# Branch B of a hybrid attention block: weights packed in another order, exponentials and rotations kept in PSUM, two of eight transposes in other banks

## What is computed

```python
qb = rms_norm(b_cq, q_a_norm_w) @ w_q_b          # 512 -> 8 heads x (128 nope + 64 rope)
qb_rope = apply_rope(qb[..., 128:], cos_b, sin_b)
kvb = rms_norm(b_ckv, kv_a_norm_w) @ w_kv_b      # 256 -> 8 heads x (128 key + 128 value)
s = (q_nope @ k_nope.T + q_rope @ k_rope.T) * scale     # block-causal, 64-token chunks
out_b = softmax(s) @ v * silu(b_g)
x = x + concat(out_a, out_b) @ w_out             # then a last rms_norm
```

## Time and profile before

| | |
|---|---|
| median of 3 runs | 711.04 us (709.88 to 712.78) |
| the profiled execution | 710.97 us; its span from first to last instruction 709.0 us |
| PE busy | 682.3 us, 96% |
| DVE, ACT, POOL busy | 317.4, 303.0, 320.4 us (45%, 43%, 45%) |
| granted TensorE clock | 0.994 of full |

### The profile page before, as it was taken

The page is one execution under the profiler, slowest core; times in us unless marked ns, Lnnn a source line. Parts: engine busy times, 40 slices in busy tenths (PEclk is TensorE's granted clock), DMA queues, the critical chain, the costliest instruction groups (busy, mean ns, idle before and its releaser), DMA issues.

```text
span 709.0 us, 9019 instructions
## 1 busy us (share of the span) xinstructions
PE 682.3 (96%) x3282; PEld 567.3 (80%) x3282; DVE 317.4 (45%) x515; ACT 303.0 (43%) x573; POOL 320.4 (45%) x150
## 2 busy tenths in 40 slices
PE   5999999999999999999999998999999999999995
PEld 4888887888888888888888786778778888888884
DVE  5977120885753633543533666675752110100013
ACT  6732232212235564564554565566553231312233
POOL 3664443444254443344243255445675385474630
PEclk9999999999999999999999999999999999999998
DMA  8632222223132122222222222210111932232215
GB/s 277 232 126 101 101 89 90 90 91 115 61 119 90 60 84 80 100 70 85 90 89 80 100 86 77 76 61 31 59 60 61 355 119 94 90 113 89 90 52 215
DMA packets 21588, 73.47 MB, mean 104 GB/s; under 512 B 2352, under 2 KB 2480, under 8 KB 21424
## 3 DMA queue, kind: packets, MB, share of 16 engines
q1 hardware_dynamic: 18144, 66.07, 26.8%
q10 hardware_dynamic: 3408, 6.90, 2.7%
HBM read 68.77 MB, written 4.19 MB: 103 GB/s over the span
## 4 chain that ended last, share of the span: by engine, by line
issue 39%; PE 32%; POOL 18%; DVE 5%; ACT 3%; DMA 1%; POOLq 0%; ACTq 0%; SPq 0%; DVEq 0%
POOL w_lo L247 18%; PE bank L956 10%; PE bank L960 10%; PE bank L959 10%; DVE t L821 1%; DVE pb L862 1%; PE bank L1168 1%; DVE st_b L854 1%; DMA xs<-x_t 1%; DVE ptb_lo L867 1%; ACT pb L481 1%; PE bank L1159 0%; PE bank L1158 0%; DMA w_raw<-w_stream 0%; DVE mixed L766 0%
## 5 line engine op out<-in xcount | busy, mean ns | idle before, releaser
L247 POOL TENSOR_TENSOR w_lo<-w_raw,w_hi 128x1024 fp32r<-128x1024 f32 x109 | 265.2, 2437 | 319.3 <-ACT w_hi L320 318.6
L320 ACT ACTIVATE w_hi<-w_raw 128x1024 fp32r<-128x1024 f32 x110 | 116.1, 1059 | 216.3 <-PE bank L956 188.4
L956 PE MATMUL bank<-x_hi,w_hi 128*128 128x512 f32 x520 | 204.8, 394 | 0.0
L960 PE MATMUL bank<-x_lo,w_hi 128*128 128x512 f32 x520 | 202.9, 390 | 0.0
L959 PE MATMUL bank<-x_hi,w_lo 128*128 128x512 f32 x520 | 202.5, 389 | 0.0
L960 PEld LDWEIGHTS bank<-x_lo,w_hi 128*128 128x128 f32 x520 | 97.6, 188 | 20.5
L956 PEld LDWEIGHTS bank<-x_hi,w_hi 128*128 128x128 f32 x520 | 97.8, 188 | 20.1 <-DVE mixed L805 0.5
L959 PEld LDWEIGHTS bank<-x_hi,w_lo 128*128 128x128 f32 x520 | 97.7, 188 | 19.7 <-issue 0.5
L956 PE MATMUL bank<-w_hi,mx_hi 128*128 128x512 f32 x256 | 101.0, 394 | 0.0
L959 PE MATMUL bank<-w_hi,mx_lo 128*128 128x512 f32 x256 | 100.0, 391 | 0.0
L960 PE MATMUL bank<-w_lo,mx_hi 128*128 128x512 f32 x256 | 99.9, 390 | 0.0
(11 more groups left out here) (177 smaller groups left out, 909.8 us busy)
## 6 DMA issues: line engine op xcount, KB each, us to landing
w_raw<-w_stream SPq DMA_DIRECT2D x110, 512.0 KB, 3.2
xs<-x_t SPq DMA_DIRECT2D x8, 512.0 KB, 4.8
y<-x_nat ACTq DMA_DIRECT2D x4, 1024.0 KB, 8.8
out<-y SPq DMA_DIRECT2D x8, 512.0 KB, 3.4
fw<-final_w ACTq DMA_DIRECT2D x1, 1024.0 KB, 15.3
cos_b<-tables ACTq DMA_DIRECT2D x2, 256.0 KB, 2.7
sin_b<-tables ACTq DMA_DIRECT2D x2, 256.0 KB, 3.0
cos_r<-tables ACTq DMA_DIRECT2D x1, 256.0 KB, 3.3
```

Source lines behind the costliest of these rows:

```text
L247: pool.tensor_tensor(w_lo[:, s % HL, :], w_raw[:, s % RAW, :], w_hi[:, s % HL, :].bitcast(F32), ALU.subtract)\
L320: act.activation(w_hi[:, s % HL, :], w_raw[:, s % RAW, :], ACT.Copy).then_inc(w_hi_ready, 1)
L956: ins = pe.matmul(dst, ah, bh, start=start, stop=False)
L960: return pe.matmul(dst, ah, bl, start=False, stop=stop)
```

## The change

- The weights of a pair are packed as (rotary queries, keys), (other queries), (values, zeros) for all pairs, and the tiles come in the order 4, 0, 3, 5, 6, 1, 2 for all pairs. Before, pair 0 had the order 4, 5, 6, 0, 3, 1, 2 and the others 0 to 6.
- Tile 4 is projected in F0 and F1, and the rotation moves from F6 to F8 of DVE's walk to F2, F3 (three operations in each) and F4. The products with the cosine and the sum are written back to the PSUM bank of tile 4; before, they went to `t1` and `t3` in SBUF. That bank is free for the next tile (tile 6) only when the two last subtractions are done (`b_rot_lo`); before, after the multiplications.
- The exponential is written back to its score bank, and N reads it there. A score bank is free after N; before, after E. So S waits for N of two blocks earlier.
- T2 of each pair goes to bank 7 and T6 to bank 5; the others stay in bank 6, and T3 and T7 wait for the D of two blocks earlier, not of the last.
- The multiplication of the last two tiles of branch A by their gate (`gate(3)`) moves from DVE (before M2 of pair 0) to POOL, ahead of a weight chunk. The DMAs of the second pair of rotation tables, which go where the gate stood, are issued on ACT in F1 of pair 0; before in F3.
- Splits (ACT and POOL) of the tiles and of the chunks move with the new order; that of tile 2 falls into F0 of the next pair.

```diff
-B_PIECES = [((0, (0, 1)),), ((1, (0, 1)),), ((2, (0, 1)),), ((3, (0, 1)),), ((4, (0, 1)),), ((4, (2, 3)),), ((5, (0, 1)),),
-            ((5, (2, 3)),), ((6, (0, 1)),), ((6, (2, 3)),), ()]
+B_PIECES = [((4, (0, 1)),), ((4, (2, 3)),), ((0, (0, 1)),), ((3, (0, 1)),), ((5, (0, 1)),), ((5, (2, 3)),), ((6, (0, 1)),),
+            ((6, (2, 3)),), ((1, (0, 1)),), ((2, (0, 1)),), ()]
-TILE_ORDER = [(4, 5, 6, 0, 3, 1, 2)] + [(0, 1, 2, 3, 4, 5, 6)] * 3
+TILE_ORDER = (4, 0, 3, 5, 6, 1, 2)
-B_SPLITS = {1: 0, 2: 1, 3: 2, 4: 3, 8: 5, 10: 6}
-B_CHUNKS = {0: 0, 5: 1, 6: 2}
-B_ROTARY = {6: 0, 7: 1}
+B_SPLITS = {3: 0, 4: 3, 6: 5, 8: 6, 9: 1}
+B_CHUNKS = {1: 0, 5: 1, 10: 2}
+B_ROTARY = {2: (0, 1, 2), 3: (3, 4, 5)}
+B_ROTARY_HIGH, B_ROTARY_LOW = 4, 5
+T_BANK = (6, 6, 7, 6, 6, 6, 5, 6)
...
             def b_expo(w):
                 u = w % 8
                 n = P * (u % 4 + 1)
-                act.wait_ge(b_turned, w + 1)
                 act.wait_ge(b_max, w + 1)
-                act.activation(pb[:, u % 4, 0:n], B[4 + u % 2][:, 0:n], ACT.Exp, bias=st_b[:, u % 4, 0:1],
+                act.activation(B[4 + u % 2][:, 0:n], B[4 + u % 2][:, 0:n], ACT.Exp, bias=st_b[:, u % 4, 0:1],
                                accum_out=st_b[:, u % 4, 2:3]).then_inc(b_exp, 1)
...
             def b_rotary(p, part):
 
+                bk, own = B[(PB_TILES * p + TILE_POS[4]) % 4], min(p, 1)
                 if part == 0:
...
-                    if p > 0:
-                        dve.wait_ge(b_rot_lo, p)
-                    dve.tensor_tensor(t1[:, :], bk[:, :], cos_b[own][:, :], ALU.mult)
-                    for q in range(4):
-                        o = q ^ 1
-                        ins = dve.tensor_tensor(t2[32 * q:32 * q + 32, :], bk[32 * o:32 * o + 32, :], sin_b[own][32 * q:32 * q + 32, :], ALU.mult)
-                    ins.then_inc(b_rot_evac, 1)
+                if part < 4:
+                    o = part ^ 1
+                    dve.tensor_tensor(t2[32 * part:32 * part + 32, :], bk[32 * o:32 * o + 32, :], sin_b[own][32 * part:32 * part + 32, :], ALU.mult)\
+                        .then_inc(b_rot_evac, 1)
+                elif part == 4:
+                    dve.wait_ge(b_rot_evac, 5 * p + 4)
+                    dve.tensor_tensor(bk[:, :], bk[:, :], cos_b[own][:, :], ALU.mult).then_inc(b_rot_evac, 1)
                 else:
-                    dve.wait_ge(b_rot_evac, p + 1)
-                    dve.tensor_tensor(t3[:, :], t1[:, :], t2[:, :], ALU.add).then_inc(b_rot, 1)
+                    dve.wait_ge(b_rot_evac, 5 * p + 5)
+                    dve.tensor_tensor(bk[:, :], bk[:, :], t2[:, :], ALU.add).then_inc(b_rot, 1)
...
-                dve.tensor_scalar(pb[:, u % 4, 0:n], pb[:, u % 4, 0:n], st_b[:, u % 4, 3:4], None, ALU.mult).then_inc(b_probs, 1)
+                dve.wait_ge(b_turned, w + 1)
+                dve.tensor_scalar(pb[:, u % 4, 0:n], B[4 + u % 2][:, 0:n], st_b[:, u % 4, 3:4], None, ALU.mult).then_inc(b_probs, 1)
...
                 if j == 4:
-                    pe.wait_ge(b_rot_evac, p + 1)
+                    pe.wait_ge(b_rot_lo, p + 1)
...
-                pe.wait_ge(b_exp, w + 1)
+                if w >= 2:
+                    pe.wait_ge(b_probs, w - 1)
+                if w % 8 == 1 and w > 1:
+                    pe.wait_ge(b_pt_lo, w - 1)
...
                 pe.wait_ge(b_probs, w + 1)
-                pe.wait_ge(b_pt_lo, w + 1)
+                if T_BANK[w % 8] == 5:
+                    pe.wait_ge(b_probs, w + 2)
+                elif T_BANK[w % 8] == 7:
+                    pe.wait_ge(b_out, w // 4 + 1)
+                    pe.wait_ge(a_out, 17)
+                elif w > 0 and T_BANK[(w - 1) % 8] != 6:
+                    pe.wait_ge(b_pt_lo, w)
+                else:
+                    pe.wait_ge(b_pt_lo, w + 1)
...
-        parts = [np.concatenate([kn, v], axis=2), np.concatenate([qr, pad], axis=2), qn]
-        stream += parts[1:] + parts[:1] if p == 0 else parts
+        stream += [np.concatenate([qr, kn], axis=2), qn, np.concatenate([v, pad], axis=2)]
```

More of the change, by code:

```diff
@@ L190, in build, with turned @@
         B = [bank(f"bank{i}") for i in range(8)]
+        def turned(w):
+            u, n = w % 8, P * (w % 4 + 1)
+            return B[T_BANK[u]][:, 0:n]
         w_landed = [sem(f"w_landed{i}") for i in range(RAW)]
@@ L273, in _ @@
                 low_part(c, c)
-            with pool.Fori(1, b_head // HL) as i:
+            with pool.Fori(1, (b_head - 1) // HL) as i:
                 for s in range(HL):
                     low_part(HL * i + s, s)
-            for c in range(b_head // HL * HL, b_head):
+            for c in range((b_head - 1) // HL * HL, b_head):
+                if c == b_head - 1:
+                    for ct in range(2):
+                        pool.wait_ge(gate_silu, 12 + ct + 1)
+                        pool.wait_ge(a_out, 12 + 5)
+                        pool.tensor_tensor(mixed[:, 6 + ct, :], mixed[:, 6 + ct, :], gate_tmp[:, ct, :], ALU.mult).then_inc(gated, 1)
                 low_part(c, c)
@@ L281, in _ @@
                 for f in range(len(B_PIECES)):
+                    if p > 0 and f == 0:
+                        b_tile_low(p, 2)
                     if p < PAIRS - 1:
@@ L505, in _ @@
             act.wait_ge(w_used, PB0)
+            b_tile_high(0, 0)
+            b_tile_high(0, 3)
+            b_rotary_high(0)
+            high_part(PB0 + AHEAD, PB0 + AHEAD)
             b_tile_high(0, 5)
-            b_rotary_high(0)
             b_tile_high(0, 6)
[L509 to L512, removed]
+            high_part(PB0 + AHEAD + 1, PB0 + AHEAD + 1)
             preload(ACT.Exp)
@@ L525, in _ @@
                     elif step[0] == "F":
-                        if p == 0 and f == 3:
+                        if p > 0 and f == 0:
+                            b_tile_high(p, 2)
+                        if p == 0 and f == 1:
                             act.wait_ge(gated, 8)
@@ L873, in b_take @@
                 dve.tensor_tensor(m, B[7][:, :], m, ALU.mult).then_inc(b_out, 1)
-            for part in range(2):
+            for part in range(6):
                 b_rotary(0, part)
-            b_tile_low(5)
+            for j in (0, 3):
+                b_tile_low(j)
             b_rotary_low(0)
-            b_tile_low(6)
-            for j in (0, 3, 1, 2):
+            for j in (5, 6, 1, 2):
                 b_tile_low(j)
@@ L905, in _ @@
                         if p < PAIRS - 1:
-                            if f in B_ROTARY:
-                                b_rotary(p + 1, B_ROTARY[f])
-                            if f == 8:
+                            for part in B_ROTARY.get(f, ()):
+                                b_rotary(p + 1, part)
+                            if f == B_ROTARY_LOW:
                                 b_rotary_low(p + 1)
@@ L915, in _ @@
                         late = None
-                    if p == 0 and step == "F" and f == 2:
-                        gate(3)
             b_take(B_HEADS - 1)
@@ L1140, in b_project @@
                     for k in ks:
-                        o = step * k + (P if j in (3, 6) else 0)
+                        o = step * k + (P if j in (3, 6) else 0) + (SEQ if j in (0, 3) else 0)
                         if p == 0 and j == 4:
@@ L1174, in b_product @@
                 pe.wait_ge(b_out, head + 1)
-                if head == 0:
-                    pe.wait_ge(a_out, 17)
-                    pe.wait_ge(b_lo, 6)
+                if head % 2 == 0:
+                    pe.wait_ge(b_lo, 6 * (head // 2) + 6)
                 for kt in range(TOK):
@@ L1199, in out_rows @@
                     ins.then_inc(o_done, 1)
-            for j in TILE_ORDER[0]:
+            for j in TILE_ORDER:
                 b_project(0, j, (0, 1) if j < 4 else (0, 1, 2, 3))
@@ L1216, in _ @@
                         if p < PAIRS - 1:
-                            if p == 0 and f == 0:
+                            if p == 0 and f == 2:
                                 pe.wait_ge(b_lo, 6)
```

54 lines of the change are left out of this document (26 added, 28 removed).

## The result

The changed kernel takes **724.32 us** (median of 4 runs, 723.46 to 724.89) against 711.91 of the kernel before in the same runs (709.88 to 712.97): a ratio of 1.0173, with a 95% interval of 1.0156 to 1.019. It is 1.7% slower. The forecast was 712.4, with a range of 704 to 717. The profiled execution is at 724.89 us with a span of 723.0.

The account below looks back on a forecast made before the run. PE bounds the kernel, so only its idle time and clock can be won. 710.97 − 12.3 (waits, clock) − 1.2 (restarts) + 12.6 (new pair waits) + 0.3 (restarts) + 2.0 (tile 6) = 712.4 us; range 704 to 717.

Parts of the forecast that it names:

- the low parts of the rotation: DVE's subtractions right behind ACT's high parts, ahead of M5, N5 and D3, to 470.05; F6 starts 1.5 us late.
- The clock: Rival, 22%: PE's clock falls in the new waits, 1.7 us at most a fall, 716 us at 1.2 in three pairs.
- The rival with 23%: DVE isn't late enough to hold PE: 706 us with half the wait per pair, 699.5 with none; chance 23%.
- under 2 us at V0: Sign meant to decide for the 23% rival: V0 waits less than 2 us in a pair.
- The old waits: PE's waits for D, 9.5 us, and for a value tile, 1.1 us, from 412 to 545 us, were to go.
- The wait at tile 6: Ahead of pair 0, tile 6 waits for the rotation's end in tile 4's bank: 1.9 us, 2.0 with restart.
- S5: In pair 1, S5 waits for the 512 wide scaling from PSUM on DVE: 0.4 us.
- S6: In pair 1, S6 waits for the 128 wide scaling behind the rotation's products and sum: 1.2 us.
- those of F6 and V0: In pair 1, F6 waits 1.5 us for the rotation's low part and V0 0.9 us for D3.
- The gate: At T1 of pair 0, the gate on DVE causes the 3.53 us wait; on POOL it was costed at nothing.
- Writing PSUM in place: Rival, 9%: in-place PSUM writes cost 0.1 to 0.25 us on 18 operations, giving 714.2 to 717 us.
- The rule of the Trainium skill: Any PSUM operand slows a float32 tensor_scalar: 512 wide scaling at 0.69 us, not 0.49; 712.4 us with it, 711.2 without.

Follow-up runs that it names:

- e2: Changed kernel with the rotation's two last subtractions in F4 instead of F5: 713.35 us, ratio 1.0025 to the kernel before.
- e10: Changed kernel with the split of tile 3 in F5, behind E5, instead of F4: 721.18 us, ratio 1.0129 to the kernel before.
- e3: Changed kernel with 16 unread 512 wide matmuls right before the wait of F6 in pairs 0 to 2: 718.16 us, ratio 1.0084 to the kernel before.
- e8: Kernel before with gate(3) on POOL, T2 in bank 7, T6 in bank 5 and the exponentials in PSUM: 702.37 us, ratio 0.9866.
- e4: Kernel before with only gate(3) moved from DVE to POOL: 708.62 us, ratio 0.9944.
- e7: Kernel before with gate(3) on POOL, T2's transposes in bank 7 and T6 in bank 5: 704.93 us, ratio 0.9906.
- e1: Changed kernel with the rotation's products back in SBUF (t1, t3): 715.68 us, ratio 1.005 to the kernel before.
- e5: Changed kernel with the exponentials back in SBUF, S waiting for E of two blocks earlier: 726.7 us, ratio 1.0213 to the kernel before.
- e9: Changed kernel with the rotation's products in SBUF and the two last subtractions in F4: 711.52 us, ratio 0.9998 to the kernel before.
- e11: Changed kernel with the split of tile 3 in F5 and the rotation's subtractions in F4: 713.85 us, ratio 1.0025 to the kernel before.

## Why the prediction was wrong

**The step that failed** is the one on the low parts of the rotation: "ACT makes the high parts of the rotation behind E4 and H2, from about 467.4, and DVE the low parts right behind". DVE does not. `B_ROTARY_LOW` is 5: the subtractions stand in F5, behind M5, N5 and D3, and not, as the section on the change has it too, in F4. The prediction sent DVE through the subtractions first and then "M5 and N5 ... and D3". In the changed kernel the order is the reverse, and F6 waits for all five. With the order that was computed, F6 waits 1.11 us and V0 0.73 (e2). With the subtractions in F5, F6 waits 3.12 (e10), and the two copies of tile 3 ahead of E5 make it 3.99. V0 then waits for nothing. A pair loses 5.5 us instead of 4.1, which is 4.2 us over three pairs.

**The clock** was a rival with 22%, "between" single waits of 1.2 and 3.5 us. With 3.99 it is no longer between. The fall came in all three pairs, twice for double the time of the earlier trace rows, and costs 6.2 us in all, tile 6 included (e3). "A fall costs 1.7 us at most" was too low for that reason. The two together are 10.4 of the 11.9 us by which the forecast of 712.4 missed. The rest is in the terms below. The rival with 23%, that DVE isn't late enough to hold PE, is out: PE waits 5.5 us a pair, and 3.4 with the order that was computed. Its sign, under 2 us at V0, couldn't have told it from the sum, which had 0.9 there itself.

**What held.** The old waits went, at T1, T2, T6, T7 and at the value tile. The wait at tile 6 is 1.88 (1.9), S5 0.37 (0.4), S6 1.15 (1.2). The walk in time order thus was the right tool. Where its list of operations was right it had the waits to 0.1 us up to S6, and in e2 those of F6 and V0 0.4 and 0.2 too long.

**What was mis-sized, and partly cancelled.** In e2 the four waits of a pair sum to 3.36 us, not 4.1, yet the time is 0.95 over the forecast. Busy time of PE in pair 2, from S0 to S0, of e2 and of e8 (columns of rows 1), shows where that went:

```profile
481.56:513.00 31.44, 28.13 (x167) 23.32 (x166) 19.63 (x43) 18.73 (x42) 17.11 (x11) 1.00 0.15 51
```

```profile
472.96:502.05 29.09, 27.56 (x165) 23.35 (x165) 20.60 (x42) 18.83 (x43) 17.38 (x10) 1.00 0.16 55
```

The same pair's work is 0.57 us longer with four waits than with two, so a restart costs 0.2 to 0.3 us, also after a short wait. The rows say where it lies: a matmul 512 wide is listed with 0.39 us though the next starts 0.23 behind it, so the idle time listed for a wait is 0.16 short of the time lost, and the second matmul behind the wait comes 0.1 late. The forecast had only that 0.1, for the twelve removed waits, and 0.3 for all twelve added ones together. By an estimate with 0.26 each, the waits were 2.2 us too long over three pairs, the added restarts 2.8 too cheap, the removed ones 1.9 too cheap, which goes the other way, and the fall at tile 6, 1.7, was left out: 0.4 of the 0.95. That the forecast lies so near e2 is in part luck, since these terms cancel.

The gate was oversized: it held T1 for 1.9 of 3.53 us (e4), and the rest goes with N0 and N1 (e7, e8). Writing PSUM in place costs next to nothing (0.70 for the DVE products against 0.69 into SBUF in e1; the exponential below), so that rival (9%) is out. The rule of the Trainium skill, "VectorE: DVE Perf Modes", section "The perf-mode tier table", held in its direction: 0.49 us at 512 from SBUF and 0.75 from PSUM, more than the 0.69 taken. It didn't decide anything: the kernel with the scaling from PSUM is the faster one, by 2.4 and 2.6 us (e5, e8).

**Where 12 us went,** from the runs: gate on POOL −2.8 (e4), transposes in other banks −3.7 (e7), exponentials in PSUM −2.6 (e8), to 702.4. Order of the tiles with the rotation ahead of M3 and M4, +9.1 (e9, 711.5). Rotation in PSUM, +1.8 (e2). Subtractions in F5 with that bank held, +11.0. By the profiled executions alone the last three are +7.3, +3.7 and +11.7, as that of e9 is one of its four shortest; the 3.7 are the wait at tile 6 and the fall behind it. Three parts of the change are worth 9.0 us, less than the 13.5 that the prediction had for all removed waits: new ones took their place (e7), and that for the value tile, 1.1, is still there in e8. The new tile order with the rotation where it now stands costs 22 us.

Not separated are the order of the tiles and the place of the rotation, as the one brings the other, and the alternation of small and large tiles was tested by no run alone. But an estimate leaves it little: the profile of e9 has 10.1 us of waits in nine places and that of e8 4.1 in five, which with 0.26 a restart makes 7.0 of the 7.3 us between the two.

## What to carry to other kernels

When an edit makes a buffer's release depend on a later instruction, write down that engine's instructions in their order up to the release and price that list; a constant that says which step it stands in can be worth more than all else (11 us here). A new wait of several microseconds on TensorE can cost its clock on top: here 6.2 us beside 13.8 of waiting. Take a change with several parts one part at a time: three of its parts (gate, banks, exponentials) made the 1.3% faster kernel, and all together were 1.7% slower.

## What the runs showed of the hardware

- **The clock after a wait.** In the traces it fell to 1.2 GHz around each wait of 3.1 us and more at F6 (three each in the changed kernel, e5 and e10), in the changed kernel for 3.4 to 6.8 us. Behind the same wait of 1.9 us at tile 6 it fell in the changed kernel, e2, e5 and e10, and not in e3 and e11. It did not behind the three waits of 1.97 at V0 in the profile of e9, nor behind 2.22 at T5 of pair 2 in e1. In e11 it fell at F6 of pair 2 behind waits of 0.36, 1.15 and 1.12. The length of one wait of up to 2.2 us does not tell.
- **Two SBUF inputs beside POOL.** 2.79 us instead of 0.69 for a VectorE subtraction (e1), and no stretching when one input is in PSUM (0.69, the changed kernel). A scaling of 128 elements takes 0.28 us to 1.82 from SBUF, 1.09 in the mean (e5), and 0.35 from PSUM. No run varied POOL's work alone, so that it is POOL is read from the timeline, not isolated.
- **The exponential into PSUM isn't slower than into SBUF.** Groups of ACT by shape, in the changed kernel:

```profile
L497 ACT ACTIVATE bank<-bank,st_b 128x512 f32<-128x512 f32 x8 | 5.3, 662 | 19.1 <-DVE st_b L872 19.1
```

  In the kernel before, into SBUF:

```profile
L481 ACT ACTIVATE pb<-bank,st_b 128x512 f32<-128x512 f32 x8 | 5.5, 689 | 12.4 <-DVE st_b L854 12.4
```
